# Means of squared query heads from high and low fp32r parts, in a two-layer hybrid trunk

## What is computed

```python
def rms_norm(x, g):
    y = xf * lax.rsqrt(jnp.mean(xf * xf, axis=-1, keepdims=True) + EPS)

proj = xn @ w_in[l]
q, k, v, u = jnp.split(proj, splits, axis=-1)
q = apply_rope(rms_norm(q, q_norm_g[l]), cos, sin) * q_scale   # 8 heads of 64
k = apply_rope(rms_norm(k, k_norm_g[l]), cos, sin)             # 2 heads of 64
attn = sliding_sink_attention(q, k, v, sinks[l])
pool = multiscale_pool(u, w_pool[l], pool_scale[l])            # trailing means, 4 groups of 128
h = h + jnp.concatenate([attn, pool], axis=-1) @ w_out[l]
```

## Time and profile before

| | us |
|---|---|
| median of 3 runs | 1055.87 (1055.59 to 1056.19) |
| the profiled execution | 1057.14 |
| its span, first to last instruction | 1054.3 |
| TensorE busy | 1037.6 (98%) |
| VectorE busy | 683.7 (65%) |
| ScalarE busy | 464.3 (44%) |
| GpSimd busy | 102.6 (10%) |
| mean granted TensorE clock | 0.997 |

### The profile page before, as it was taken

One profiled execution on the slowest core, in us unless ns is written; L12 is line 12 of the kernel. 1 busy time (PEld: TensorE's weight loads), 2 busy tenths in 40 slices (PEclk: granted clock), 3 DMA queues, 4 the chain that ended last, 5 costly groups with the idle time before them and its releaser, 6 DMA issues.

```text
span 1054.3 us, 18706 instructions
## 1 busy us (share of the span) xinstructions
PE 1037.6 (98%) x7880; PEld 991.5 (94%) x7880; DVE 683.7 (65%) x1018; ACT 464.3 (44%) x706; POOL 102.6 (10%) x108
## 2 busy tenths in 40 slices
PE   7999999999999999999999999999999999999998
PEld 7998999999999999999999889999889998899987
DVE  6668644569945599455546784555797557975452
ACT  6886535434423343233338773443442334422322
POOL 1253000110001100011002510000000000000000
PEclk9999999999999999999999999999999999999999
DMA  7211332222333222322231203233223332232212
GB/s 236 81 52 40 96 105 81 81 82 80 106 99 116 81 81 81 121 81 90 82 109 51 81 2 121 81 100 100 80 81 121 91 109 81 78 122 88 95 60 80
DMA packets 94106, 94.94 MB, mean 90 GB/s; under 512 B 3424, under 2 KB 92856, under 8 KB 94024
## 3 DMA queue, kind: packets, MB, share of 16 engines
q1 hardware_dynamic: 93456, 93.58, 27.7%
q10 hardware_dynamic: 312, 0.18, 0.1%
q0 software_dynamic: 256, 0.01, 0.0%
HBM read 91.65 MB, written 2.10 MB: 89 GB/s over the span
## 4 chain that ended last, share of the span: by engine, by line
PE 83%; DVE 9%; ACT 4%; issue 2%; DMA 1%; SPq 0%; DVEq 0%; ACTq 0%
PE slot L567 64%; PE slot L961 11%; PE slot L772 2%; PE slot L616 1%; DVE w_lo L420 1%; PE slot L1021 1%; ACT sumsq L1231 1%; DMA x_in<-in_x 1%; DVE h L1925 1%; PE slot L832 1%; PE slot L839 1%; DVE ms_work L1620 1%; PE slot L804 1%; DVE k_dup L1632 1%; DVE nmax L1683 1%
## 5 line engine op out<-in xcount | busy, mean ns | idle before, releaser
L567 PE MATMUL slot<-x_hi,w_hi 128*128 128x264 f32 (+2 forms) x1516 | 354.9, 301 | 1.0 <-DVE w_lo L420 0.6
L567 PE MATMUL slot<-x_lo,w_hi 128*128 128x264 f32 (+2 forms) x1516 | 350.5, 298 | 0.0
L567 PE MATMUL slot<-x_hi,w_lo 128*128 128x264 f32 (+2 forms) x1516 | 350.2, 298 | 0.0
L567 PEld LDWEIGHTS slot<-x_hi,w_hi 128*128 128x128 f32 x1516 | 246.5, 189 | 12.6 <-issue 1.4
L567 PEld LDWEIGHTS slot<-x_lo,w_hi 128*128 128x128 f32 x1516 | 245.1, 189 | 7.3
L567 PEld LDWEIGHTS slot<-x_hi,w_lo 128*128 128x128 f32 x1516 | 244.8, 189 | 7.5
L420 DVE TENSOR_TENSOR w_lo<-raw,w_hi 128x2048 fp32r<-128x2048 f32 (+2 forms) x68 | 151.7, 2230 | 98.8 <-ACT w_hi L409 98.8
L409 ACT ACTIVATE w_hi<-raw 128x2048 fp32r<-128x2048 f32 (+2 forms) x68 | 124.0, 1823 | 150.5 <-PE slot L567 95.4
L1125 POOL TENSOR_TENSOR work<-work 128x528 f32<-128x528 f32 (+1 forms) x32 | 41.8, 1308 | 707.1 <-DVE work L1849 348.6
L1407 ACT ACTIVATE work<-gate,par_all 128x528 f32<-128x528 f32 (+1 forms) x44 | 31.9, 730 | 134.8 <-DVE gate L1576 67.8
L961 PE MATMUL slot<-m_op_hi,w_hi 128*128 128x264 f32 (+1 forms) x256 | 73.8, 288 | 1.2 <-DVE h L1925 0.8
(11 more groups left out here) (212 smaller groups left out, 1666.9 us busy)
## 6 DMA issues: line engine op xcount, KB each, us to landing
raw<-in_w_gate SPq DMA_DIRECT2D x44, 512.0 KB, 4.5
raw<-in_w_up SPq DMA_DIRECT2D x44, 512.0 KB, 4.4
raw<-in_w_down SPq DMA_DIRECT2D x32, 512.0 KB, 4.5
raw<-in_w_in SPq DMA_DIRECT2D x19, 512.0 KB, 4.7
raw<-in_w_out SPq DMA_DIRECT2D x16, 512.0 KB, 4.2
raw<-in_w_down SPq DMA_DIRECT2D x16, 384.0 KB, 3.6
x_in<-in_x SPq DMA_DIRECT2D x4, 512.0 KB, 6.9
out<-y_out SPq DMA_DIRECT2D x4, 256.0 KB, 2.3
```

What stands on the lines that cost most here:

```text
L567: ins = nc.tensor.matmul(out_part, w[ws][:, r, cols], a[:, k, tokens], start=first and n == 0 and w is w_hi and a is a_hi, stop=end and w ...
```

## The change

Each squared query block is split into a high and a low fp32r part, and two fp32r matmuls (high, then low, into the same PSUM columns) take the place of the one in full fp32. The high part is a ScalarE copy (`squares_hi`), the low part a VectorE subtraction (`squares_lo`). Blocks 1 to 8 are kept in `pool_hi` and `pool_lo`, which the pooling uses only later; block 0 has buffers of its own. The two constant columns are copied once into an fp32r tile, `pair_mean`. q_squares(2) waits for the low parts of kv 0 where it waited for the means. squares_hi(0) stands ahead of shift(3) and squares_hi(1) ahead of the high split of `U_U01`; squares_lo(0) behind sine_part(3) and squares_lo(1) behind sine_part(4). On TensorE the means stand later among the pooling rows.

```diff
 def q_means(kv, b0, b1):
-                        pe.wait_ge(headsq_ready, l * 5 + (2 * kv + 3))
+                        pe.wait_ge(pair_ready, 1)
+                        pe.wait_ge(sqlo_ready, 2 * l + kv + 1)
                     for b in range(b0, b1):
-                        ins = nc.tensor.matmul(slot[s][:, 0, 2 * b:2 * b + 2], head_sq[:, b, :],
-                                               cst[:, C_BLK:C_BLK + P:HEAD_DIM], start=True, stop=True)
+                        for n in range(2):
+                            ins = nc.tensor.matmul(slot[s][:, 0, 2 * b:2 * b + 2], square_block(n, b), pair_mean[:],
+                                                   start=n == 0, stop=n == 1)
...
-                u3_rows(0, 1)
+                u3_rows(0, 5)
                 q_means(0, 0, 3)
-                u3_rows(1, 2)
+                u3_rows(5, 6)
                 q_means(0, 3, 6)
-                u3_rows(2, 3)
+                u3_rows(6, 7)
                 q_means(0, 6, 9)
-                u3_rows(3, 7)
                 fill(0, 2)
                 u3_rows(7, 8)
-                fill(2, 4)
+                fill(2, 8)
                 q_means(1, 0, 3)
-                fill(4, 5)
+                fill(8, 9)
                 q_means(1, 3, 6)
-                fill(5, 6)
+                fill(9, 10)
                 q_means(1, 6, 9)
                 scores(0)
-                fill(6, 8)
+                fill(10, 11)
                 scores(1)
-                fill(8, 14)
+                fill(11, 14)
                 scores(2)
...
                     if j == 2:
-                        act.wait_ge(filled[ps.slot("qn0")], ps.before("qn0", l) + 1)
+                        act.wait_ge(sqlo_ready, 2 * l + 1)
...
+                def squares_hi(kv):
+                    act.wait_ge(headsq_ready, l * 5 + (2 * kv + 3))
+                    if kv == 1:
+                        act.wait_ge(filled[ps.slot("qn0")], ps.before("qn0", l) + 1)
+                    nc.scalar.activation(sq_meta[0][:], head_sq[:, 0], ACT.Copy)
+                    nc.scalar.activation(sq_real[0], head_sq[:, 1:].rearrange("p b q -> p (b q)"), ACT.Copy)\
+                      .then_inc(sqhi_ready, 1)
...
                 if l == 0:
+                    nc.scalar.activation(pair_mean[:], cst[:, C_BLK:C_BLK + P:HEAD_DIM], ACT.Copy).then_inc(pair_ready, 1)
...
+                squares_hi(0)
                 shift(3)
                 q_squares(2)
                 q_rms(0)
                 shift(4)
                 q_squares(3)
+                squares_hi(1)
                 split_hi(act, l, U_U01)
...
+                def squares_lo(kv):
+                    dve.wait_ge(sqhi_ready, 2 * l + kv + 1)
+                    nc.vector.tensor_tensor(sq_meta[1][:], head_sq[:, 0], sq_meta[0][:].bitcast(f32), ALU.subtract)
+                    nc.vector.tensor_tensor(sq_real[1], head_sq[:, 1:].rearrange("p b q -> p (b q)"),
+                                            sq_real[0].bitcast(f32), ALU.subtract).then_inc(sqlo_ready, 1)
...
-                for j in (2, 3):
-                    q_tile(j)
-                    sine_part(j + 1)
+                q_tile(2)
+                sine_part(3)
+                squares_lo(0)
+                q_tile(3)
+                sine_part(4)
+                squares_lo(1)
```

More of the change, by code:

```diff
@@ L159, in build_trunk @@
         eps = sb(ctx, "eps", [P, 1])
+        pair_mean = sb(ctx, "pair_mean", [P, 2], f32r)
         with ExitStack() as sc:
@@ L180, in build_trunk @@
             q_scale = sb(sc, "q_scale", [P, NB, 2, N_KV_HEADS])
+            sq_meta = [sb(sc, f"sq_meta_{n}", [P, 2 * CHUNK], f32r) for n in ("hi", "lo")]
             sine = v_T[:]
@@ L260, in build_trunk @@
         headsq_ready = sem("headsq_ready")
+        sqhi_ready, sqlo_ready, pair_ready = sem("sqhi_ready"), sem("sqlo_ready"), sem("pair_ready")
         headn_ready = sem("headn_ready")
@@ L298, in build_trunk, with square_block @@
         HALF_TILES = [(g, half) for g in GROUPS[1:] for half in range(2)]
+        sq_real = [t[:].rearrange("p a t -> p (a t)")[:, 0:2 * SEQ] for t in (pool_hi, pool_lo)]
+        def square_block(n, b):
+            return sq_meta[n][:] if b == 0 else sq_real[n][:, (b - 1) * 2 * CHUNK:b * 2 * CHUNK]
         def half_name(kind, g, half):
```

## The result

The changed kernel takes 1077.07 us (1075.29 to 1078.10, five runs) against 1055.87 (1055.59 to 1056.97, five runs) for the kernel before beside it: a ratio of 1.0196 [1.0185, 1.0208], 21.2 us slower. The profiled execution took 1077.24, with a span of 1075.3 against 1054.3, so its trace holds the whole loss of 21.0 us in the span. TensorE comes to the second layer's stage 9.65 us late (the matmul that starts at 576.21 in the kernel before starts at 585.86), so 9.65 us belong to the first layer and 11.35 to the second.

The account below looks back on a forecast made before the run. Two bounds side by side: TensorE's work and the ScalarE/VectorE chain to pool_lo. Delays of +7.0 us a layer, 14.0 in all, plus 0.2 for the pair_mean copy, on 1057.14 give 1071.3, less 1.3: 1070.0; range 1063 to 1076.

Parts of the forecast that it names:

- A batch of six pairs at 0.68: Means on TensorE: six load-and-matmul pairs for three blocks take 0.68 us in fp32r as before, so no gain.
- The late case: squares_lo(0) on VectorE: GpSimd's q_rot addition goes first, low parts ready at 59.8 us instead of 58.6; shift(4) +3.0.
- the 1.9 for the slow clock: TensorE's last two rows and two batches before the first maxima: 2.1 us of work takes up to 4.0 at 1.2 GHz.
- What comes back: First maxima to the first pool_hi row: fewer VectorE steps held by GpSimd give back 1.0 us at full clock, 2.2 at half.
- half-clock case: TensorE's resumption at the pool_hi row: its own work ends last, at 87.0 (88.1) us, +6.9 (+8.0) a layer.
- the paragraph on the clock: TensorE's restart at the u2b row, 72.1 (73.2): expected at 1.2 GHz after 5.5 us idle with one small batch between.
- the second layer repeats the first: Both layers' stages: the second repeats the first 521.42 us later, so +7.0 a layer is doubled to 14.0.
- more slow clock: Rival: the first idle 1.1 us also slows kv 0's means, 1 to 2 us a layer, 1073 to 1075; chance 0.10.
- Cheap means: Rival on TensorE's means: fp32r loads of half the length take 1.7 us a layer off, 1066.6; chance 0.12.
- faster: Case on TensorE's means: half-length loads where TensorE alone sets the pace, 1055.9 - 4.1 = 1051.8 us; chance 0.05.
- fill(8,9) not binding: Rival at u2b's first row: u3's evacuation comes before TensorE, means end about 2.8 us earlier, 1063 to 1064; chance 0.07.
- Full clock: Rival: TensorE's clock stays full after the idle time, +4.8 to +5.9 us a layer, 1066.5; chance 0.20.

Follow-up runs that it names:

- the swap: Kernel before with squares written as fp32r and two fp32r matmuls a block replacing the fp32 one, no low parts, old order: 1055.99 us, ratio 1.0004.
- The spare matmuls: Changed kernel plus matmuls nobody reads in TensorE's idle places (8 before kv 0's means, 23 before kv 1's, 20 before the first u2b row): 1069.25 us.
- the order alone: Kernel before with only TensorE's new order, full-fp32 means, no high and low parts: 1071.82 us; with idle places filled by unread matmuls 1064.38 us.
- The single matmul: Kernel before with squares written as fp32r and one fp32r matmul a block, half of the means' loads, no low parts: 1055.84 us, ratio 0.9999.

## Why the prediction was right and wrong

Forecast were 1070.0 and a range from 1063 to 1076; it took 1077.07, just above the range. The direction, the waits and their places were right, the size was not.

**The means.** A batch of six pairs at 0.68: measured 0.66 (59.75 to the next pooling row at 60.41) and 1.40 a batch with its row in the swap alone. The Trainium skill ("FP8 and Floating Point Precision", TensorE Precision Notes) gives full fp32 four passes. The trace records two load-and-matmul pairs, and two fp32r ones in their place change nothing at two columns: the swap has a ratio of 1.0004. The Trainium skill ("TensorE: Matmul & The Clock Gate", Weight-path perf modes) gives a fast weight load to 128 weights whose type isn't FP32. It did not show for fp32r here: the pairs stay at 0.11 us.

**VectorE against GpSimd.** The late case held: low parts at 59.61 (59.8 forecast), the subtraction 2.31 us long beside GpSimd's addition and 1.22 alone. The Trainium skill ("SBUF — State Buffer", Who interferes with whom) says that a VectorE instruction with two SBUF inputs contends with a GpSimd instruction that reads SBUF, and that the order of issue decides who is blocked. The trace agrees: GpSimd had started 0.11 us earlier, and VectorE took 1.09 us longer.

**The chain.** shift(4) at 63.8, measured 63.70. High split at 68.3, measured 68.30. Idle time of 2.8 before kv 1, measured 2.88; 2.7 before the u2b row, measured 2.43. u3 evacuated at 73.2, measured 73.21. Last means at 77.2 with a slow clock, measured 77.3, and the first maxima 78.44, against 76.15 and the 1.9 for the slow clock. Each of these terms stood.

**The step that failed is "What comes back", in its half-clock case**, with the paragraph on the clock ahead of it: the stretch at 1.2 GHz was put far too short. It had one slow stretch: 2.1 us of means doubled to 4.0, and then 10.9 us from scores(0) to the pool_hi row, in which, by the kernel before's own rows, only some 3 us are slow. Measured, the clock stayed at 1.2 GHz from 70.54 to 84.19, 13.65 us, and scores(0) to that row took 89.30 - 77.29 = 12.0. That gives +9.2 where the half-clock case had +8.0, and I had then taken +7.0, between the cases; with what the heads' longer wait adds (0.5) the layer ends 9.65 late, 2.65 more than forecast. That the second layer repeats the first did not hold either: it loses 11.35, another 1.7, of which 1.4 come from the stretch at half clock over the means of kv 0. 14.0 + 2 x 2.65 + 1.7 = 21.0, the loss in the span.

The spare matmuls show that it is the clock: filling the idle time brings 7.8 us back (7.4 on the order alone) though the parts that TensorE waits for come no earlier in their chain. The nearest rival, "more slow clock", named the means of kv 0 and gave 1 to 2 us a layer. That happened in the second layer alone, where it cost 1.4. The rival had the right mechanism, but left out that the stretch behind kv 1 would be long too, and its end of 1075 was still short.

**The rivals.** Cheap means: refuted by the batch of the swap, 1.40 us with its row. The single matmul shows more, that in the kernel before even half of the loads would have gained nothing, which also answers the case "faster"; whether the 1.7 us a layer that I gave the rival would have come in the changed kernel, where the means hold q_rms(0), no run shows. fill(8,9) not binding: refuted by its 2.43 us. Full clock: not what happened, but measured with the spares at 1069.25, some 3 us above the 1066.5 that I gave it.

## What to carry to other kernels

In a stage where TensorE's work and a chain of ScalarE and VectorE steps are equally long, look for what a later step holds up behind it in each queue: here two instructions that cost nothing themselves, a root ahead of a rotation and a filling row that needed another engine's evacuation, made 14.5 of 21.2 us. When you forecast new idle time on TensorE of a few microseconds, add the slow clock as a term of its own, with an upper bound well beyond the stretches that the trace of before shows: here waits of 11.2 us came with slow matmuls that cost 7.8 us on top. And test a claim like that with spare matmuls in the idle time, before taking the waits apart.

## What the hardware showed that I had not expected

The low level of the clock lasted far longer than the trace of before let me expect: 3.4 us a layer there, where it cost nothing; in the changed kernel 13.65 in the first layer and 6.8 + 10.2 in the second; and the whole 13.4 us looked at with the order alone. In these long stretches TensorE was busy 11.07 of 13.50 us, and in one 10.10 of 10.10, while the granted clock read 0.50.

Idle time is not the only thing that stands ahead of a fall. In the kernel before the clock fell at 68.12 and 590.36, and TensorE had no wait in the stage ahead of either:

```profile
58.00:68.10 10.10, 10.10 (x89) 1.00 0.01 2
580.00:590.30 10.30, 10.30 (x92) 1.00 0.00 0
```

What stood there were the two-column means of kv 1 and the first scores. That idle time brought most of the slow time in the changed kernel, but not all of it, is what its spare matmuls show: of 30.7 us at half clock in the two stages 3.4 are left.

The low level also differed between the layers of one execution: the first ran the means of kv 0 at full clock, the second at half, with 1.05 and 1.03 us of idle time before them. What decides between the two was not tested.
